# Attention projections 3 and 4 of a float32 decoder trunk with the 512-wide moving operand, and VectorE's sums placed ahead of the weight halves in the feed-forward chunks

## The reference, cut to what matters

```python
def swiglu(x, w_gate, w_up, w_down):
    return (jax.nn.silu(x @ w_gate) * (x @ w_up)) @ w_down      # 1024 -> 2816 -> 1024

def mixer_attention(x, w_in, b_f, w_out, rel_bias):
    h = x @ w_in                                # 1024 -> 3080: q, k, v of 8 + 8 heads, and 8 forget logits
    ...
    o_a = moba_attention(qkv_a[0], qkv_a[1], qkv_a[2], rel_bias)      # softmax(q k^T / 8 + bias) v, causal
    o_b = forgetting_attention(qkv_b[0], qkv_b[1], qkv_b[2], log_f)   # softmax(q k^T / 8 + c_t - c_s) v, causal
    o = jnp.concatenate([o_a, o_b], axis=1).transpose(0, 2, 1, 3).reshape(B, S, D_ATTN)
    return o @ w_out
```

## Time and profile before

| what | value |
|---|---|
| median of 3 runs | 1004.65 us (1004.18 to 1005.0) |
| the profiled execution | 1004.67 us, span of its records 1002.9 us |
| PE busy | 995.8 us, 99% of the span |
| DVE, ACT busy | 705.1 us (70%), 453.5 us (45%) |
| granted TensorE clock | 1.0 of full speed |
| DMA | 191.60 MB, mean 191 GB/s |

### The profile page before, as it was taken

One profiled execution on the slowest core, in us unless ns is written; L12 is line 12 of the kernel. 1 busy time (PEld: TensorE's weight loads), 2 busy tenths in 40 slices (PEclk: granted clock), 3 DMA queues, 4 the chain that ended last, 5 costly groups with the idle time before them and its releaser, 6 DMA issues.

```text
span 1002.9 us, 13745 instructions
## 1 busy us (share of the span) xinstructions
PE 995.8 (99%) x5260; PEld 846.4 (84%) x5260; DVE 705.1 (70%) x870; ACT 453.5 (45%) x520; POOL 41.8 (4%) x55
## 2 busy tenths in 40 slices
PE   9999999999999999999999999999999999999998
PEld 7788888889877888888888888888888888888887
DVE  5676666767788776667687666767788867667674
ACT  5544344245564543434356343434344553434441
POOL 0400000100001000000010000000210000000010
PEclk9999999999999999999999999999999999999999
DMA  9965656455336766555449555554466676555531
GB/s 297 295 221 168 208 168 209 126 170 181 112 117 223 257 203 208 171 206 181 155 158 307 207 175 202 181 198 169 151 193 231 217 245 210 174 202 181 197 126 42
DMA packets 129692, 191.60 MB, mean 191 GB/s; under 512 B 5448, under 2 KB 95816, under 8 KB 129520
## 3 DMA queue, kind: packets, MB, share of 16 engines
q1 hardware_dynamic: 126432, 180.11, 54.4%
q0 software_dynamic: 2928, 10.61, 3.1%
q10 hardware_dynamic: 288, 0.26, 0.1%
HBM read 189.90 MB, written 1.06 MB: 190 GB/s over the span
## 4 chain that ended last, share of the span: by engine, by line
PE 91%; DVE 3%; DMA 3%; ACT 1%; SPq 1%; issue 1%; DVEq 0%; ACTq 0%
PE gu L597 23%; PE gu L605 12%; PE acc L419 9%; PE acc L420 9%; PE acc L421 9%; PE gu L419 7%; PE gu L421 7%; PE gu L420 7%; PE tp L514 2%; DMA rawA<-in_ffn_w_up 2%; PE gu L825 2%; PE gu L806 1%; DVE g_lo L1276 1%; DMA bias_tab<-in_ffn_w_up 1%; PE gu L830 1%; PE gu L809 1%
## 5 line engine op out<-in xcount | busy, mean ns | idle before, releaser
L597 PE MATMUL gu<-xT,g_hi 128*128 128x512 f32 x1024 | 243.4, 390 | 0.8 <-DVE stage L1450 0.8
L597 PEld LDWEIGHTS gu<-xT,g_hi 128*128 128x128 f32 x1024 | 191.9, 188 | 40.6 <-DVE stage L1448 1.2
L1276 DVE TENSOR_TENSOR g_lo<-rawA,g_hi 128x2048 fp32r<-128x2048 f32 (+2 forms) x65 | 139.1, 2143 | 76.6 <-ACT g_hi L962 76.5
L1068 ACT ACTIVATE stage<-stage 128x256 f32<-128x256 f32 x64 | 26.8, 418 | 262.6 <-DVE stage L1448 262.6
L1276 DVE TENSOR_TENSOR g_lo<-rawB,g_hi 128x2048 fp32r<-128x2048 f32 (+1 forms) x64 | 138.7, 2169 | 9.3 <-ACT g_hi L962 9.1
L962 ACT ACTIVATE g_hi<-rawA 128x2048 fp32r<-128x2048 f32 (+2 forms) x66 | 118.1, 1794 | 51.2 <-DMA rawA<-in_ffn_w_up 21.9
L419 PE MATMUL acc<-d_hi,hT_hi 128*128 128x512 f32 x352 | 139.4, 396 | 0.0
L420 PE MATMUL acc<-d_lo,hT_hi 128*128 128x512 f32 x352 | 138.0, 392 | 0.0
L421 PE MATMUL acc<-d_hi,hT_lo 128*128 128x512 f32 x352 | 137.4, 390 | 0.0
L605 PEld LDWEIGHTS gu<-xT,g_lo 128*128 128x128 f32 x1024 | 131.3, 192 | 5.0
L419 PE MATMUL gu<-g_hi,xT 128*128 128x512 f32 x336 | 133.1, 396 | 0.0
(11 more groups left out here) (200 smaller groups left out, 986.8 us busy)
## 6 DMA issues: line engine op xcount, KB each, us to landing
rawD<-in_ffn_w_down SPq DMA_DIRECT2D x44, 1024.0 KB, 4.9
rawA<-in_ffn_w_gate SPq DMA_DIRECT2D x42, 512.0 KB, 4.0
rawA<-in_ffn_w_up SPq DMA_DIRECT2D x42, 512.0 KB, 4.9
rawB<-in_ffn_w_gate SPq DMA_DIRECT2D x42, 512.0 KB, 3.9
rawB<-in_ffn_w_up SPq DMA_DIRECT2D x42, 512.0 KB, 5.0
rawA<-in_attn_w_in SPq DMA_DIRECT2D x12, 512.0 KB, 4.6
rawB<-in_attn_w_in SPq DMA_DIRECT2D x12, 512.0 KB, 4.9
rawA<-in_ple_w_gate SPq DMA_DIRECT2D x8, 512.0 KB, 4.9
```

Of the source, the lines that this page charges most:

```text
L597: pe.matmul(bank[:, :], g_hi[:, slot, b, at:at + P], xT[:, b, :, :].rearrange("p i t -> p (i t)"), start=b == 0, stop=False)
L1068: act.activation(stage[:, i_f, 0:S], stage[:, i_f, 0:S], ACT.Silu).then_inc(act_done, 1)
L1276: return dve.tensor_tensor(dst, src, hi.bitcast(F32), ALU.subtract)
```

## The change

`WIDE` goes from 2 to 4, so chunks 3 and 4 go through `qk_wide` too, with a row for each of their halves in `WIDE_STEPS`. The scale of the queries (1/8) moves into the weights of chunk 3, as it was with chunk 1. ACT no longer copies q and k of chunks 3 and 4; DVE makes them by eight more sums. In the feed-forward loop DVE does both sums of a half ahead of the low part of the weights, and not behind it.

```diff
-WIDE = 2
-WIDE_STEPS = {(1, 0): ("low", 0, 1), (1, 1): (0, 1, "low"), (2, 0): (0, 1, "low"), (2, 1): (0, "low", 1)}
+WIDE = 4
+WIDE_STEPS = {(1, 0): ("low", 0, 1), (1, 1): (0, 1, "low"), (2, 0): (0, 1, "low"), (2, 1): (0, "low", 1),
+              (3, 0): ("low", 0, 1), (3, 1): (0, 1, "low"), (4, 0): (0, 1, "low"), (4, 1): (0, 1, "low")}
@@ ACT, attention
-                            elif c == 0 and WIDE:
-                                hi_scaled(g0 + 1, h)
+                            elif c in (0, 2):
+                                hi_scaled(g0 + c + 1, h)
@@ DVE, feature_chunk
                             gates, h = stage[:, i_f, 0:S], stage[:, i_f, S:2 * S]
-                            lo_g_into(c + (g0 + 1), slot, i_f)
                             dve.wait_ge(gate_full, m + i_f + 1)
                             dve.tensor_reduce(gates, gu[0][:, :].rearrange("p (i t) -> p t i", i=2), AXX, ALU.add).then_inc(gate_sum, 1)
                             dve.wait_ge(g_done, 2 * c + (2 * g0 + i_f + 1))
                             dve.tensor_reduce(h, gu[1][:, :].rearrange("p (i t) -> p t i", i=2), AXX, ALU.add).then_inc(up_sum, 1)
+                            lo_g_into(c + (g0 + 1), slot, i_f)
@@ DVE, attention
-                            elif c == 0 and WIDE:
+                            elif c == 0:
                                 lo_scaled(g0 + 1, h)
                             elif 1 <= c <= WIDE:
                                 for part in WIDE_STEPS[c, h]:
                                     if part == "low":
-                                        lo_g(g0 + c + 1, h)
+                                        (lo_scaled if c == 2 else lo_g)(g0 + c + 1, h)
                                     else:
                                         qk_sum(c, h, part)
```

## The result

The changed kernel takes 1007.59 us (median of 8 runs, 1007.3 to 1008.05), the kernel before 1004.78 in the same rounds. The ratio is 1.0027, with a 95% interval of 1.0018 to 1.0036. The change makes the kernel slower by 2.8 us. The profiled execution has 1007.3 us, with a span of 1005.6.

What follows compares the result with a forecast made beforehand. PE was taken as the bound in both changed places. From 1004.67 us, +4.2 for the attention stage (wide-form gain included) and -0.9 for the feed-forward wait gave 1008.0 us, range 1005.8 to 1010.0.

Steps and rivals of the forecast that it cites:

- Part 1: Four attention halves of chunks 3 and 4 turn wide on PE: at most 0.84 us less PE work.
- Step (a): First half of chunk 3: PE waits 0.9 us for bank gu1, freed by DVE's second sum of ("g", 2, 1).
- Step (b): Before chunk 3's second half: PE waits 1.3 us for the gu0 sum behind chunk 4's DMA-delayed low half.
- Step (c): DVE's in-order queue: 2.3 us late at the rawB low half, 4.5 at the last low half of chunk 4.
- Step (d): Probabilities: PE waits about 1.2 us at heads 4 and 5, 1.6 at 6 and 7, ending about 4.2 late.
- the attention part: Wide halves of chunks 3 and 4 and their bank waits together: +4.2 us, bounds +3.0 and +4.7.
- Part 3: Feed-forward sums ahead of low halves: the one PE wait near 47 us goes, -0.93 us, no second gain.
- the covers: Feed-forward: PE work hides the later low halves, hT_lo and rawB reload; tightest at block ends, 0.3 us left.
- DVE in pace: Rival: DVE finishes sums whenever PE returns for the bank, only gains remain: 1002.9 us; chance 0.14.
- Early weights of chunk 4: Rival: chunk 4's weights land early, removing the 1.3 us wait before chunk 3's second half: 1006.8 us; chance 0.12.
- late block ends: Rival: moved operations 0.8 us later than worked out, PE waits 0.5 in each of four feed-forward blocks: 1010.0; chance 0.08.

Runs made afterwards that it cites:

- all moves: Changed kernel with both sums before the low half for (2, 1), (3, 0), between-sums low halves in chunk 4, cumulative operation later, second inverse earlier: 1003.73 us.
- the feed-forward order alone: Changed kernel with WIDE back at 2, so only the feed-forward edit against the kernel before: 1003.54 us, ratio 0.9993.
- The two rows tried one at a time: Changed kernel with both sums ahead of the low half in one table row: ("g", 2, 1) took 1007.37 us, ("g", 3, 0) took 1006.58.
- The idle sums: Kernel with only the feed-forward edit, plus two unused DVE sums behind each low half of chunks 3 and 4: 1011.73 us; in the real sums' shape 1008.11.
- the row of ("g", 3, 0): Changed kernel with both sums of chunk 3's first half ahead of chunk 4's low half: 1006.58 us, ratio 1.0024.
- the versions at 1003.5 to 1004.3: Feed-forward edit only 1003.54; all four chunks wide, DVE queue rearranged 1003.73; both rows changed, cumulative operation late 1004.21; only chunk 3 newly wide, queue eased 1004.31 us.

## Why the prediction was right, point by point

**The whole.** 1008.0 was forecast and 1007.59 measured, with the mechanism that was named: DVE's queue late, PE waiting for it, and one wait less in the feed-forward. The forecast was +3.3 and the result +2.8. By the trace 0.1 of the 0.5 between them lies in the stage (4.1 for 4.2) and 0.4 ahead of it (1.29 for 0.9).

**Part 1, the wide form on PE.** Right in kind, and a little too large. A wide half free of waits takes 246.04 - 240.36 = 5.68 us against 5.85. That is 0.17 for each half (0.19 in ("g", 4, 0)) and 0.7 in all, where the prediction had at most 0.84. Its 0.21 came from ("g", 2, 1), which takes 5.63 in after as well. Why the later halves gain 0.05 less was not tried. The estimate from the Trainium skill ("TensorE: Matmul & The Clock Gate", back-to-back issue gap), 0.16 us in all, is far from these 0.7 in after, and the trace decides. The formula behind it is given there for an isolated matmul; the same section says that in a stream of weight loads and matmuls, as here, both set the spacing. So the prediction's sentence that by the page the wide form is worth almost nothing holds for that formula alone. But with DVE nearly in pace (all moves against the feed-forward order alone) only 65.82 - 65.73 = 0.1 us of them reached the end of the stage, since the wait that was left (0.3 in its bracket) cost 0.5.

**Step (a).** The wait for bank gu1 is there, 0.71 in its bracket. The half is 0.80 longer, and with the 0.17 that the form gains the wait cost 0.97 (forecast 0.9).

**Step (b).** 1.31 by the spacing, 1.24 in the bracket (forecast 1.3). The two rows tried one at a time show that (a) is not a loss of its own. Without it PE comes earlier to (b) and waits there longer by about as much. The forecast added both, which is right in sum, since (b) is a moment (DVE's late weights) and not a length.

**Step (c).** DVE was to be 2.3 late at the low half of rawB, and is 2.4. It stands at 246.85, or 248.14 in the time of before, where the forecast was 248.0 and the row of before 245.72. At the reciprocal of head 7 it is 269.79, in that time 271.08 (forecast 271.1). The idle sums show by themselves that such lateness costs PE time: 4.1 us with the halves of chunks 3 and 4 narrow.

**Step (d).** By the spacing the two stretches with the probabilities lose 1.09 and 1.39. With the 0.18 of the wide half the first is 1.27. The forecast had 1.2 and 1.6. The brackets show 0.71 and 1.13, so that whoever adds brackets would find 3.8 for all waits, where the spacings give 0.97 + 1.31 + 1.27 + 1.39 = 4.9. Less the 0.7 of the wide halves and the 0.13 around ("g", 4, 0), the attention part was +4.1 (forecast +4.2).

**Part 3.** The wait near 47 is gone. PE's next half starts at 46.42 for 47.49, 1.07 earlier, of which 0.14 was there already at the last down matmul (46.19 for 46.33). That leaves 0.93, as forecast. The term was mis-sized in one thing. At ("g", 2, 1) after is 1.29 earlier, not 0.93: 0.14 is there ahead of the edit's place, and 0.2 builds up behind it. The 0.14 is luck of this execution: with the feed-forward order alone the last down matmul stands at 46.43, 0.10 later than before, and ("g", 2, 1) starts 1.01 earlier. Behind the wait that kernel gains 0.2 too (46.66 to 225.87, where before has 47.49 to 226.88), so this part seems to come with the edit. What it is made of was not traced. None of the covers failed. At the block's end 0.4 us were left (forecast 0.3), and in a steady half the sums stand at once behind their banks:

```profile
413.47 0.69 DVE L1448 TENSOR_REDUCE stage<-gu 128x256 f32<-128x512 f32 x1 [1.56 <-PE gu L606]
...
414.43 0.69 DVE L1450 TENSOR_REDUCE stage<-gu 128x256 f32<-128x512 f32 x1 [0.27 <-PE gu L606]
...
415.04 2.28 DVE L1277 TENSOR_TENSOR g_lo<-rawB,g_hi 128x2048 fp32r<-128x2048 f32 x1
416.98 3.34 PE L598 MATMUL gu<-xT,g_hi 128*128 128x512 f32 x14
```

Against the earlier trace rows the low half has moved behind the sums, and PE's next half follows without a gap.

**The rivals.** DVE in pace is refuted for this order, and true of another: with all moves its mechanism is there, yet at 1003.7 and not the 1002.9 that it gave. Early weights of chunk 4 did not come by themselves; the row of ("g", 3, 0) does the same to step (b) and gives 1006.6, where this rival said 1006.8. The late block ends did not come.

**Open.** Whether any of the versions at 1003.5 to 1004.3 beats the kernel before is not settled: each interval holds 1. The traces favour the feed-forward order alone by 1.0 us over the kernel before (PE's start of ("g", 2, 1)).

## What to carry to other kernels

Work that moves from an engine with slack to one with an in-order queue is not paid by its duration or by the busy share, but by what stands behind it: follow the lateness to the next thing that the bounding engine needs, even 30 us on. If removing one wait gives nothing, look for the moment that another engine's data set; the same time is then waited a few us later. Read a wait's cost from the spacing of starts on the waiting engine, in both kernels, and take the bracket as a lower bound.

## What the runs showed of the hardware that was not expected

- A wait costs PE more than its bracket. A matmul of 512 columns has a record of 0.39 us at a spacing of 0.227, so behind such matmuls 0.16 of a wait hides under the last record. At the probabilities of heads 4 and 5 more is hidden: the six transposes behind the wait took 1.14 us from their start to the next product, against 0.74 before (262.09 to 262.83), with no bracket between them. The four places cost 4.9 us against 3.8 in brackets.
- A DVE reduction's time depends on its form, not only on what it reads. From 128x512 inputs in the same buffer, 256 sums of 2 took 0.70 us and 64 sums of 8 took 1.06. The two forms also differ in how far apart the addends lie, and that was not tried separately.
